# Turning expert rows on VectorE in 32x32 blocks, and one-hot products in plain fp32

## The chip, the cores and the metric

The kernel runs on one core of one Trainium2 chip. The metric is the device time of one execution, in microseconds, from the first to the last instruction and what lies around them.

## The reference

The program is two blocks, each on 512 tokens of width 1024. The first is a hybrid layer (block-sparse attention and a gated delta rule), the second a pair of token mixers followed by a layer of product-key experts. Only the last layer is touched by the change, and the norm and projection ahead of it:

```python
def peer(xn, w_q, sub_keys, u_tab, v_tab):        # u_tab, v_tab: (16384, 1024)
    q = (t @ w_q).reshape(n_tok, PEER_HEADS, 2, PEER_HALF)
    sc = jnp.einsum("thpk,hpnk->thpn", q, sub_keys)
    s_top, i_top = lax.top_k(sc, PEER_TOPK)
    ...                                           # 16 best of 16 x 16 candidates: idx, softmax g
    ue = u_tab[ib]                                # 128 rows of u for each token
    act = jax.nn.gelu(jnp.einsum("phkd,pd->phk", ue, tb))
    return jnp.einsum("phk,phkd->pd", gb * act, v_tab[ib])
```

There are 16384 experts, 128 x 128, and each token uses 128 of them (8 heads of 16).

## The kernel before

For three of the four groups of 128 tokens (384 tokens, `DENSE`) the kernel does not gather. It multiplies all experts' rows with the tokens: `u @ x` for each of 128 tiles of 128 experts, then GELU, then weighs the result with a dense table of the gate weights ("spread": experts x tokens, mostly zero), and multiplies by `v`. The last group of 128 tokens takes its rows by indirect DMA from GpSimd, one row for each token at a time, and VectorE makes the dot product with the token ("dot", 128 of them).

All large products are made of three fp32r products: an operand is split in a high part (rounded to fp32r) and a low part (the rest), and high x high, low x high and high x low are added.

The first 24 expert tiles are multiplied inside `choose_experts`, beside the top-k search. There TensorE turns a tile (8 transposes of 128x128, L1721), ScalarE copies it from PSUM twice (L1782, L1783), GpSimd makes the low part (L1832), TensorE multiplies (L1755).

The stage around the change is the first part of `expert_products`, the first expert product: 104 tiles, in rounds of four (`PER`). For tile u the steps are: SyncE loads 128 rows of 4 KB (L2058); TensorE turns them into two PSUM banks (`turn`, L2186); ScalarE writes the high part (`high`, L2401), VectorE the low part (`low`, L2260); TensorE makes 8 x 3 products of 384 columns (`multiply`, L2205); ScalarE applies GELU (L2435) and issues the store of the result (L2439).

In the first 96 tiles each tile has also one step of the spread, 4 tokens: VectorE compares key numbers with the tokens' chosen keys (`one`, L2267, and `match`, L2268), GpSimd multiplies `match` by the gate weights, high and low part (`two`, L2128), TensorE multiplies `one` and `two` (L2194), ScalarE copies the high half from PSUM into `spread` (L2408) and VectorE adds the low half (L2275). GpSimd stores finished chunks of 64 tokens to memory in 8 pieces (L2142), in half of the tiles. VectorE makes 5 dots in a round (L2280).

Each engine runs its own list in program order and waits on semaphores; there is no planner. TensorE's list is turn(u+1), multiply(u), spread step u. ScalarE's is high(u+1), GELU and store of u, spread copy of u. VectorE's is low(u+1), one-hots of u+1, dot, spread add of u. `after(n)` is n plus the one that every semaphore starts with. The second expert product (L2222, from 1662 us) and the end follow in the same block.

Of the kernel before, what the change touches and what calls it, by code (L numbers as in the profile page):

```python
# [6 lines left out]
F32 = mybir.dt.float32  # L7
# [7 lines left out]
P = 128  # L15
# [117 lines left out]

class NormAndTurn:
# [4 lines left out]
    def __init__(self, nc, k, tag, out, weight, xs, stat, rooted=False):  # L139

        self.k, self.out, self.w0, self.xs, self.stat, self.rooted = k, out, COLS[weight][0], xs, stat, rooted
        self.vec, self.sq, self.root, self.scaled, self.turned, self.his, self.los = (
            k.sem(f"{tag}_{n}") for n in ("vec", "sq", "root", "scaled", "turned", "hi", "lo"))
# [37 lines left out]
    def tensor(self, pe):  # L181
        k = self.k
        for t in range(TT):
            pe.wait_ge(self.scaled, t + 1)
            for c in range(DC):
                mm = pe.transpose(k.ps[c][:, t * P:(t + 1) * P], self.xs[t][:, c * P:(c + 1) * P], k.ident[:, :])
                if t == TT - 1:
                    mm.then_inc(self.turned, 1)
# [5 lines left out]
def project_first(nc, k, io, src, w8, proj, gates, z_raw):  # L194
# [11 lines left out]
    with ExitStack() as st:  # L206
# [18 lines left out]
        def steps_of(eng, body):  # L225
# [16 lines left out]
            k.sem(n) for n in ("rows_in", "other_rows_in", "w8_in", "ident_zero", "ident_done", "row_made", "values_set", "rows_turned", "cols_done"))  # L242

# [14 lines left out]
        with nc.Block() as block:  # L258
            @block.sync
            def _(sp):  # L260
# [1312 lines left out]
def choose_experts(nc, k, io, src, raw, chosen, rows, residual, acts, early_out):  # L1573
# [7 lines left out]
    w_dram = io["peer_wq_2"][0].rearrange("(c p) n -> p c n", p=P)  # L1581
# [8 lines left out]
    with ExitStack() as st:  # L1590
# [27 lines left out]
        u_dram = io["peer_u_2"][0].rearrange("(p c) d -> p c d", c=NKEYS)  # L1618
        flat_half = lambda ap, n: ap[:, 4 * n:4 * n + 4, :].rearrange("p c n -> p (c n)")
# [29 lines left out]
        norm = NormAndTurn(nc, k, "k_norm", src, "norm2", xs, k.norm_stat, rooted=True)  # L1649
        with nc.Block() as block:  # L1650
            @block.sync
            def _(sp):
# [18 lines left out]
                for e in range(EARLY):  # L1671
# [3 lines left out]
                    if e == EARLY - 3:  # L1675
                        sp.wait_ge(s["reduced"], after(steps))
                        for n in range(2):
                            sp.dma_start(k.xh[:, 2 + n, :], u_dram[:, EARLY + n, :]).then_inc(u_next_in, 16)
                sp.wait_ge(s["residual_out"], after(16))
                sp.wait_ge(u_next_in, after(32))  # L1680
# [4 lines left out]
            def _(pe):  # L1685
# [28 lines left out]
                def turn(e):  # L1714
# [5 lines left out]
                    for c in range(DC):  # L1720
                        mm = pe.transpose(k.ps[c // 4][:, c % 4 * P:(c % 4 + 1) * P], u_raw[e % 2][:, c * P:(c + 1) * P],  # L1721
# [239 lines left out]
def expert_products(nc, k, io, src, chosen, rows, acts, early_out, weights, spread, residual, out):  # L1961
# [8 lines left out]
    u_dram = io["peer_u_2"][0].rearrange("(p c) d -> p c d", c=NKEYS)  # L1970
# [5 lines left out]
    with ExitStack() as st:  # L1976
# [3 lines left out]
        two = [k.sb(f"u_two{b}", [P, TOK_TILE, 2, P], F32R, ctx=st) for b in range(2)]  # L1980
        match = k.sb("u_match", [P, TOK_TILE, P], ctx=st)
        weight_hi = k.sb("u_weight_hi", [P, DENSE], F32R, ctx=st)
        weight_lo = k.sb("u_weight_lo", [P, DENSE], ctx=st)
# [596 lines left out]
```

## Time and profile before

| | |
|---|---|
| median of 3 runs | 2200.09 us (2199.28 to 2201.86) |
| span of the profiled execution | 2200.7 us; the page gives no other time for it |
| mean granted TensorE clock | 0.983 |
| `choose_experts` | about 840 to 1087 us |
| first expert product, 104 tiles | 1087 to 1662 us |
| second expert product and end | 1662 to 2201 us |

A row of the timeline gives start, duration, engine, line, operation, output and inputs, and a count where like instructions are merged. Instructions of one engine overlap a little, so the distance of two starts is what one costs its engine. A plain fp32 matmul is recorded as two.

### The profile page before, as it was taken

The numbers are of one execution on the slowest core, as the hardware profiler recorded it, in microseconds if no ns is written. First come the engines' busy times: TensorE is split into PE (matmuls) and PEld (weight loads), VectorE is DVE, ScalarE is ACT, GpSimd is POOL, SyncE is SP. The second block draws the span as 40 slices with busy tenths as digits, with TensorE's granted clock in tenths as the row PEclk, the third lists the DMA queues.
The fourth block names the chain that finished last, engine by engine and source line by source line (L and its number), as shares of the span: only waits on it lengthen the run. The fifth ranks groups of instructions, "written<-read, shape, count | busy, mean of one in ns | idle before, by whom it ended". The sixth has DMA issues, their size and how long they took to land.

```text
span 2200.7 us, 35703 instructions
## 1 busy us (share of the span) xinstructions
PE 2099.8 (95%) x11175; PEld 1853.1 (84%) x11175; DVE 1692.5 (77%) x3372; ACT 828.2 (38%) x1439; POOL 773.6 (35%) x672
## 2 busy tenths in 40 slices
PE   6998988979999998999899999999999999999997
PEld 4886788758888877899899999999998888888886
DVE  3776555677778744999688888888877888888887
ACT  4454423522323224244444444444433333333333
POOL 2000044500000000334478988988743222222221
PEclk9999989989999999999999999999999999999999
DMA  6743100405234224124477988988789999999995
GB/s 136 94 59 39 20 1 20 133 14 138 69 96 111 79 82 158 58 80 142 165 245 255 320 292 285 315 284 298 256 297 343 342 335 339 338 338 338 336 340 197
DMA packets 229811, 428.46 MB, mean 195 GB/s; under 512 B 18500, under 2 KB 155876, under 8 KB 229476
## 3 DMA queue, kind: packets, MB, share of 16 engines
q1 hardware_dynamic: 173108, 255.96, 38.5%
q0 software_dynamic: 41472, 151.01, 19.9%
q10 hardware_dynamic: 15152, 20.51, 2.6%
q8 instruction: 40, 0.66, 0.1%
q14 instruction: 39, 0.32, 0.0%
HBM read 381.28 MB, written 46.14 MB: 194 GB/s over the span
## 4 chain that ended last, share of the span: by engine, by line
PE 48%; DMA 1%; DVE 1%; POOL 0%; issue 0%; SPq 0%; ACT 0%; DVEq 0%; POOLq 0%
PE bank L2222 22%; PE bank L2205 20%; PE bank L2186 4%; PE bank L2194 2%; DMA v_gg<-weights 1%; DMA acts<-u_weight_lo 0%; POOL row_slot L1957 0%; DVE u_spread L2380 0%; DVE v_residual L2370 0%; POOL u_two L2128 0%; DVE u_lo L2339 0%; DVEq L2051 0%; SPq L2066 0%; ACT u_spread L2471 0%; SPq L2062 0%
## 5 line engine op out<-in xcount | busy, mean ns | idle before, releaser
L2222 PE MATMUL bank<-u_hi,u_one 128*128 128x512 f32 x768 | 299.1, 389 | 1.6 <-DVE u_two L2342 1.5
L2222 PE MATMUL bank<-u_lo,u_one 128*128 128x512 f32 x768 | 298.8, 389 | 0.0
L2222 PE MATMUL bank<-u_hi,u_two 128*128 128x512 f32 x768 | 298.8, 389 | 0.0
L2205 PE MATMUL bank<-xt_hi,u_hi 128*128 128x384 f32 x832 | 287.1, 345 | 0.0
L2205 PE MATMUL bank<-xt_hi,u_lo 128*128 128x384 f32 x832 | 279.0, 335 | 0.0
L2205 PE MATMUL bank<-xt_lo,u_hi 128*128 128x384 f32 x832 | 278.7, 335 | 0.0
L1957 POOL DMA_INDIRECT row_slot<-in_peer_v_dram,row_index x128 | 141.1, 1102 | 388.0 <-DVE row_x L2350 365.3
L2416 ACT ACTIVATE u_hi<-xh 128x1024 fp32r<-128x1024 f32 x128 | 135.9, 1061 | 330.4 <-PE bank L2222 329.8
L2339 DVE TENSOR_TENSOR u_lo<-xh,u_hi 128x1024 fp32r<-128x1024 f32 x128 | 156.8, 1225 | 78.8 <-ACT u_hi L2416 76.0
L1641 POOL TENSOR_TENSOR k_wlo<-q_raw,k_whi 128x2048 fp32r<-128x2048 f32 x4 | 18.7, 4683 | 467.0 <-ACT k_whi L1769 467.0
L2128 POOL TENSOR_TENSOR u_two<-u_match,u_weight_hi 128x512 fp32r<-128x512 f32 x96 | 162.3, 1691 | 50.7 <-DVE u_match L2268 49.7
L1514 PE MATMUL bank<-xt_hi,x_whi 128*128 128x512 f32 x448 | 177.8, 397 | 1.6 <-DVE xt_lo L178 0.9
L1957 POOL DMA_INDIRECT row_slot<-in_peer_u_dram,row_index x128 | 160.1, 1250 | 50.8 <-issue 34.1
L1514 PE MATMUL bank<-xt_hi,x_wlo 128*128 128x512 f32 x448 | 174.4, 389 | 0.0
L1514 PE MATMUL bank<-xt_lo,x_whi 128*128 128x512 f32 x448 | 174.3, 389 | 0.0
L2222 PEld LDWEIGHTS bank<-u_hi,u_one 128*128 128x128 f32 x768 | 144.1, 188 | 32.7 <-DVE u_lo L2339 2.3
L2222 PEld LDWEIGHTS bank<-u_lo,u_one 128*128 128x128 f32 x768 | 144.2, 188 | 30.0
L2222 PEld LDWEIGHTS bank<-u_hi,u_two 128*128 128x128 f32 x768 | 144.1, 188 | 29.9
L2435 ACT ACTIVATE xh<-bank 128x384 f32<-128x384 f32 x102 | 50.2, 492 | 315.4 <-PE bank L2205 282.0
L2350 DVE SCALAR_TENSOR_TENSOR row_x<-row_slot,row_dot,row_x 128x1024 f32<-128x1024 f32 x128 | 163.7, 1279 | 0.0
L2280 DVE SCALAR_TENSOR_TENSOR row_slot<-row_slot,row_x 128x1024 f32<-128x1024 f32 x128 | 160.6, 1257 | 0.0
L2205 PEld LDWEIGHTS bank<-xt_lo,u_hi 128*128 128x128 f32 x832 | 156.9, 189 | 0.0
(440 smaller groups left out, 4947.2 us busy)
## 6 DMA issues: line engine op xcount, KB each, us to landing
xh<-in_peer_v_dram SPq DMA_DIRECT2D x128, 512.0 KB
xh<-in_peer_u_dram SPq DMA_DIRECT2D x104, 512.0 KB, 4.5
x_raw<-in_w_in_dram SPq DMA_DIRECT2D x56, 512.0 KB, 6.9
v_ga<-acts SPq DMA_DIRECT2D x128, 192.0 KB
acts<-xh ACTq DMA_DIRECT2D x102, 192.0 KB
weights<-u_spread POOLq DMA_DIRECT2D x32, 512.0 KB
v_gg<-weights SPq DMA_DIRECT2D x128, 128.0 KB
p_raw<-in_w_in_dram SPq DMA_DIRECT2D x12, 1024.0 KB, 10.2
```

Of the source, the lines that this page charges most:

```text
L1514: mm = pe.matmul(k.ps[n][:, :], w[n][:, c, :], x[:, c, :], start=(c == 0 and w is whi and x is hi), stop=(c == DC - 1 and w is wlo))
L1957: pool.indirect_dma_start(rows["slots"][slot][:, :], None, io_rows, bass.IndirectOffsetOnAxis(ap=rows["index"][:, n:n + 1], axis=0)).then_ ...
L2128: pool.tensor_tensor(two[b][:, :, h, :], match[:, :, :], part.unsqueeze(2).to_broadcast([P, TOK_TILE, P]), ALU.mult).then_inc(two_done, 1)
L2186: mm = pe.transpose(k.ps[2 * b + f][:, c % 4 * P:(c % 4 + 1) * P], raw[b][:, c * P:(c + 1) * P], k.ident[:, :])
L2194: mm = pe.matmul(k.ps[6 + q // 2][:, q % 2 * 2 * P:(q % 2 + 1) * 2 * P], one[b][:, q, :], two[b][:, q, :, :].rearrange("p h n -> p (h n)") ...
L2205: mm = pe.matmul(k.ps[4 + b][:, 0:DENSE], w[b][:, c, :], x[:, c, 0:DENSE], start=(c == 0 and w is uhi and x is hi), stop=(c == DC - 1 and ...
L2222: mm = pe.matmul(k.ps[q][:, :], h[b][:, t * P:(t + 1) * P], w[b][:, f], start=start and h is hhi and w is vhi, stop=stop and h is hlo, ski ...
L2280: dve.scalar_tensor_tensor(out=rows["slots"][slot][:, :], in0=rows["slots"][slot][:, :], scalar=1.0, in1=rows["x"][:, :], op0=ALU.mult, op ...
L2339: dve.tensor_tensor(vlo[b], v_raw[u], vhi[b].bitcast(F32), ALU.subtract).then_inc(slot_v[u], 1)
L2350: dve.scalar_tensor_tensor(out=total_of[:, :], in0=rows["slots"][u][:, :], scalar=rows["dot"][:, bass.ds(n * PER + u, 1)], in1=total_of[:, ...
L2416: act.activation(vhi[b], v_raw[u], ACT.Copy).then_inc(v["vhi_done"][b], 1)
L2435: act.activation(to, k.ps[4 + b][:, 0:DENSE], ACT.Gelu_apprx_tanh).then_inc(s["ga_done"][b], 1)
```

## The change

1. Rows are loaded in four DMAs, one for each quarter of the features (`load_turnable`): partition a*32+r gets, for each of four groups q of 32 experts, 256 features of expert row r. VectorE turns 32x32 blocks (`turn`), and its output `ut` has feature 8p+c on partition p of chunk c. So everything that is multiplied with it uses every eighth feature: the norm's turn of the tokens, the query weights, the gain columns of norm2 (loaded anew at the end of the first stage's SyncE list), and the turns of the 24 early tiles (`every_eighth`). `turn` runs two tiles ahead of the product.
2. `high` and `low` read `ut` in SBUF, one instruction each and not two.
3. `two` is plain fp32: ScalarE multiplies `match` by the weight, one copy of 128 columns for each of the four tokens (`scaled_matches`). TensorE's one-hot products are plain fp32, 128 columns, and come before the tile's product. ScalarE alone copies the result (`keep_spread`, 512 columns).
4. GpSimd only gathers and stores.

The core of the diff (the changed buffers and the waits at the switch to the second product are left out, as are the parameters that only carry the stride):

```diff
+def every_eighth(x, c):
+    return x.rearrange("p (q c) -> p c q", c=DC)[:, c, :]
+
+def load_turnable(eng, to, u_quarters, at, sem):
+    for a in range(4):
+        part = u_quarters[a][:, :, at, :].rearrange("r q o m -> r q (o m)")
+        eng.dma_start(to[a * 32:(a + 1) * 32, :].rearrange("r (q m) -> r q m", q=4), part).then_inc(sem, 16)
...
+                at, n = COLS["norm2"]
+                sp.wait_ge(cols_done, 2)
+                sp.dma_start(k.cols[:, at:at + n], io["norm2_g_2"].rearrange("a (p c) -> p (a c)", c=DC)).then_inc(norm2_in, 16)
+                sp.wait_ge(norm2_in, 16)
...
-    w_dram = io["peer_wq_2"][0].rearrange("(c p) n -> p c n", p=P)
+    w_dram = io["peer_wq_2"][0].rearrange("(p c) n -> p c n", p=P)
...
+        u_quarters = io["peer_u_2"][0].rearrange("(q r c) (a m) -> a r q c m", q=4, r=32, a=4)
...
-                        mm = pe.transpose(k.ps[c // 4][:, c % 4 * P:(c % 4 + 1) * P], u_raw[e % 2][:, c * P:(c + 1) * P],
+                        mm = pe.transpose(k.ps[c // 4][:, c % 4 * P:(c % 4 + 1) * P], every_eighth(u_raw[e % 2], c),
...
-                    sp.wait_ge(s["turned"][b], after(before * 2))
-                    sp.dma_start(raw[b], u_dram[:, bass.ds((n * PER + (u + EARLY)) % EXPERT_TILES, 1), :].rearrange("p a d -> p (a d)")
-                                 ).then_inc(s["raw_in"][b], 16)
+                    sp.wait_ge(s["turned"][b], after(before))
+                    load_turnable(sp, raw[b], u_quarters, bass.ds((n * PER + (u + EARLY)) % EXPERT_TILES, 1), s["raw_in"][b])
...
                 def spread_tokens(step, b):
                     pe.wait_ge(one_done, after(step + 1))
-                    pe.wait_ge(two_done, after(step * 2 + 2))
-                    pe.wait_ge(spread_kept, after(step * 2))
+                    pe.wait_ge(two_done, after(step + 1))
+                    pe.wait_ge(spread_kept, after(step))
                     for q in range(TOK_TILE):
-                        mm = pe.matmul(k.ps[6 + q // 2][:, q % 2 * 2 * P:(q % 2 + 1) * 2 * P], one[b][:, q, :],
-                                       two[b][:, q, :, :].rearrange("p h n -> p (h n)"), start=True, stop=True)
+                        mm = pe.matmul(k.ps[6 + b][:, q * P:(q + 1) * P], one[b][:, q, :].bitcast(F32), two[b][:, q, :],
+                                       start=True, stop=True)
...
                     for u in range(PER):
-                        if ahead(n, u):
-                            turn(n, u + 1)
-                        multiply(n, u)
                         if c is not None:
                             spread_tokens(n * PER + u, u % 2)
+                        multiply(n, u)
...
+                def turn(n, u):
+                    b, before = place(n, u)
+                    dve.wait_ge(s["raw_in"][b], after(before * 64))
+                    dve.wait_ge(s["hi_done"][b], after(before))
+                    dve.wait_ge(s["lo_done"][b], after(before))
+                    dve.transpose(ut[b].rearrange("p c (q r) -> p q c r", q=4),
+                                  raw[b].rearrange("p (q j c) -> p q c j", q=4, c=DC)).then_inc(s["turned"][b], 1)
+
                 def low(n, u):
                     b, before = place(n, u)
...
+                    dve.wait_ge(s["hi_done"][b], after(before + 1))
+                    dve.tensor_tensor(ulo[b][:, :, :], ut[b], uhi[b][:, :, :].bitcast(F32), ALU.subtract).then_inc(s["lo_done"][b], 1)
+
+                def onehots(step, b):
+                    dve.wait_ge(spread_ready, after(step - 1) if not isinstance(step, int) else max(step, 1))
+                    dve.tensor_tensor(one[b][:, :, :], keys, picks(step_at(step), 0), ALU.is_equal).then_inc(one_done, 1)
+                    dve.wait_ge(two_done, after(step))
+                    dve.tensor_tensor(match[:, :, :], keys, picks(step_at(step), 1), ALU.is_equal).then_inc(match_done, 1)
...
                     for u in range(PER):
+                        turn(n, u + 2)
                         low(n, u + 1)
...
+                        onehots(n * PER + (u + 1), (u + 1) % 2)
+                        dot(n * SLOTS + u, u, n + 1)
                     dot(n * SLOTS + PER, PER, n + 1)
...
                 def high(n, u):
                     b, before = place(n, u)
+                    act.wait_ge(s["turned"][b], after(before + 1))
                     act.wait_ge(s["product"][b], after(before))
...
+                    act.activation(uhi[b][:, :, :], ut[b], ACT.Copy).then_inc(s["hi_done"][b], 1)
+
+                def scaled_matches(step, b):
+                    act.wait_ge(match_done, after(step + 1))
+                    act.wait_ge(spread_ready, after(step - 1) if not isinstance(step, int) else max(step, 1))
+                    for q in range(TOK_TILE):
+                        at = slice(step * TOK_TILE + q, step * TOK_TILE + q + 1) if isinstance(step, int) else bass.ds(step * TOK_TILE + q, 1)
+                        ins = act.activation(two[b][:, q, :], match[:, q, :], ACT.Copy, scale=chosen[:, 2, at])
+                    ins.then_inc(two_done, 1)
+
+                def keep_spread(c, step, b):
                     act.wait_ge(spread_ready, after(step + 1))
...
+                    slots = bass.ds(step * TOK_TILE + (c % 2 * CHUNK - c * CHUNK), TOK_TILE)
+                    act.activation(spread[:, :, slots], k.ps[6 + b][:, :].rearrange("p (q n) -> p n q", q=TOK_TILE), ACT.Copy
+                                   ).then_inc(spread_kept, 1)
...
                         else:
                             act.wait_ge(spread_ready, after(steps))
                             split(0, 0)
+                        if c is not None:
+                            keep_spread(c, n * PER + u, u % 2)
+                            scaled_matches(n * PER + (u + 1), (u + 1) % 2)
                         b, before = place(n, u)
                         act.wait_ge(s["product"][b], after(before + 1))
```

## Rows read from the trace of the kernel before

**Rows 1.** The page: busy time, share of the span and instructions of each engine.
```profile
PE 2099.8 (95%) x11175; PEld 1853.1 (84%) x11175; DVE 1692.5 (77%) x3372; ACT 828.2 (38%) x1439; POOL 773.6 (35%) x672
```

**Rows 2.** The chain of waits, 1290 to 1320: start, us, what.
```profile
1296.76 0.47 PE bank L2194 x4
1297.23 0.87 PE bank L2186 x8
1298.11 4.17 PE bank L2205 x24
```

**Rows 3.** Waits of the stage, 1087 to 1665: us in total, times, longest.
```profile
PE bank L2194 <- POOL u_two L2128: 1.8, 1, 1.8
```

**Rows 4.** The timeline of ScalarE, last eight tiles: start, us, instruction.
```profile
1633.06 0.49 ACT L2435 ACTIVATE xh<-bank 128x384 f32<-128x384 f32 x1 [2.99 <-PE bank L2205]
...
1634.03 1.09 ACT L2401 ACTIVATE u_hi<-bank 128x512 fp32r<-128x512 f32 x2 [0.48 <-PE bank L2186]
...
1639.08 1.09 ACT L2401 ACTIVATE u_hi<-bank 128x512 fp32r<-128x512 f32 x2 [0.47 <-PE bank L2186]
```

**Rows 5.** The timeline of TensorE at an earlier stage's scores.
```profile
941.44 1.05 PE L1702 MATMUL bank<-k_t,k_qt 128*128 128x128 f32 x8
942.25 0.48 PE L1694 MATMUL bank<-xt_hi,k_whi 128*128 128x512 f32 x1
942.56 0.40 PE L1694 MATMUL bank<-xt_lo,k_whi 128*128 128x512 f32 x1
```

**Rows 6.** The timeline, second expert product.
```profile
1799.67 1.06 ACT L2416 ACTIVATE u_hi<-xh 128x1024 fp32r<-128x1024 f32 x1 [2.55 <-PE bank L2222]
...
1800.76 1.23 DVE L2339 TENSOR_TENSOR u_lo<-xh,u_hi 128x1024 fp32r<-128x1024 f32 x1 [0.60 <-ACT u_hi L2416]
...
1801.91 0.55 DVE L2342 TENSOR_TENSOR u_two<-v_h,u_one 128x384 fp32r<-128x384 f32 x1
```

**Rows 7.** The timeline, one tile of the first expert product.
```profile
1302.12 0.64 PE L2194 MATMUL bank<-u_two,u_one 128*128 128x256 f32 x4
...
1302.91 0.40 ACT L2408 ACTIVATE u_spread<-bank 128x256 f32 x1
...
1303.19 0.39 ACT L2408 ACTIVATE u_spread<-bank 128x256 f32 x1
...
1305.49 0.69 DVE L2267 TENSOR_TENSOR u_one<-row,chosen 128x512 fp32r<-128x512 f32 x1
...
1306.10 0.69 DVE L2268 TENSOR_TENSOR u_match<-row,chosen 128x512 f32<-128x512 f32 x1
```

**Rows 8.** The timeline of ScalarE, copies with a pointer scale.
```profile
288.89 1.14 ACT L846 ACTIVATE proj<-bank,d_small 128x128 f32 x4 [1.09 <-PE bank L886]
289.90 0.61 ACT L849 ACTIVATE x_raw<-bank 128x512 f32 x1
```

**Rows 9.** Groups of instructions: busy us, mean ns of one, idle before.
```profile
L2186 PEld LDWEIGHTS bank<-ident,xh 128*128 128x128 f32 x832 | 96.1, 143 | 4.5 <-issue 4.4
...
L1915 DVE SCALAR_TENSOR_TENSOR xh<-k_rank,k_top_f 128x256 f32<-128x256 f32 x64 | 44.8, 849 | 0.5
```

**Rows 10.** The timeline of VectorE, two dots in a row.
```profile
1635.87 1.22 DVE L2280 SCALAR_TENSOR_TENSOR row_slot<-row_slot,row_x 128x1024 f32<-128x1024 f32 x1
...
1637.01 1.22 DVE L2280 SCALAR_TENSOR_TENSOR row_slot<-row_slot,row_x 128x1024 f32<-128x1024 f32 x1
```

**Rows 11.** Stretches: length; busy (instructions) of each engine; granted clock, DMA share, GB/s.
```profile
1095.00:1101.00 6.00, 4.82 (x23) 4.83 (x24) 4.61 (x9) 1.89 (x5) 4.30 (x5) 0.72 0.94 364
1131.00:1175.00 44.00, 44.00 (x289) 44.00 (x289) 37.55 (x69) 18.19 (x40) 35.58 (x27) 1.00 0.75 251
1207.80:1251.90 44.10, 44.10 (x289) 44.10 (x288) 38.73 (x69) 18.16 (x40) 41.05 (x32) 1.00 0.98 334
```

**Rows 12.** The page, DMA issues: count, KB each, us to landing.
```profile
q_raw<-in_peer_u_dram SPq DMA_DIRECT2D x24, 512.0 KB, 3.6
q_raw<-in_peer_wq_dram SPq DMA_DIRECT2D x8, 1024.0 KB, 5.6
```

More of the change, by code:

```diff
@@ L2013, in place, with picks @@
             return u % 2, n * half + u // 2
-        def places(c, step, m):
-            slots = bass.ds(step * TOK_TILE + (2 * m - c * CHUNK + c % 2 * CHUNK), 2)
-            return spread[:, :, slots], k.ps[6 + m][:, :].rearrange("p (q h n) -> p h n q", q=2, h=2)
+        def picks(at, n):
+            return chosen[:, n, at].unsqueeze(2).to_broadcast([P, TOK_TILE, P])
+        keys = k.row[:, :].unsqueeze(1).to_broadcast([P, TOK_TILE, P])
+        step_at = lambda step: bass.ds(step * TOK_TILE, TOK_TILE) if not isinstance(step, int) else slice(step * TOK_TILE, (step + 1) * TOK_TILE)
         v_raw = [k.xh[:, u, :] for u in range(PER)]
@@ L2120, in _ @@
                 u_rows = io["peer_u_2"][0]
-                def weigh(step):
-                    b, tok = step % 2, slice(step * TOK_TILE, (step + 1) * TOK_TILE)
-                    pool.wait_ge(match_done, after(step + 1))
-                    if step >= 2:
-                        pool.wait_ge(spread_ready, after(step - 1))
-                    for h, part in enumerate((weight_hi[:, tok].bitcast(F32), weight_lo[:, tok])):
-                        pool.tensor_tensor(two[b][:, :, h, :], match[:, :, :], part.unsqueeze(2).to_broadcast([P, TOK_TILE, P]),
-                                           ALU.mult).then_inc(two_done, 1)
                 def fetch(n):
@@ L2240, in _ @@
                 for b in range(2):
[L2241 removed]
+                    pe.wait_ge(s["lo_done"][b], after(uses))
                 for u in range(PER):
@@ L2257, in low @@
                     b, before = place(n, u)
-                    for f in range(2):
-                        dve.wait_ge(s["hi_done"][b], after(before * 2 + (f + 1)))
-                        dve.tensor_tensor(ulo[b][:, 4 * f:4 * f + 4, :], k.ps[2 * b + f][:, :].rearrange("p (c n) -> p c n", c=4),
-                                          uhi[b][:, 4 * f:4 * f + 4, :].bitcast(F32), ALU.subtract).then_inc(s["lo_done"][b], 1)
-                def onehots(at, b):
-                    keys = k.row[:, :].unsqueeze(1).to_broadcast([P, TOK_TILE, P])
-                    picks = lambda n: chosen[:, n, at].unsqueeze(2).to_broadcast([P, TOK_TILE, P])
-                    dve.tensor_tensor(one[b][:, :, :], keys, picks(0), ALU.is_equal).then_inc(one_done, 1)
-                    dve.tensor_tensor(match[:, :, :], keys, picks(1), ALU.is_equal).then_inc(match_done, 1)
@@ L2270, in keep @@
-                def keep(c, step):
-                    for m in range(2):
-                        dve.wait_ge(high_kept, after(step * 2 + (m + 1)))
-                        to, parts = places(c, step, m)
-                        dve.tensor_tensor(to, to, parts[:, 1, :, :], ALU.add).then_inc(spread_kept, 1)
+                    dve.wait_ge(s["hi_done"][b], after(before + 1))
+                    dve.tensor_tensor(ulo[b][:, :, :], ut[b], uhi[b][:, :, :].bitcast(F32), ALU.subtract).then_inc(s["lo_done"][b], 1)
@@ L2297, in late_rounds @@
                     for u in range(PER):
+                        if ahead(n, u, 2):
+                            turn(n, u + 2)
                         if ahead(n, u):
@@ L2446, in _ @@
                 high(0, 0)
+                scaled_matches(0, 0)
                 for n in range(2, 4):
```

91 lines of the change are left out of this document (30 added, 61 removed).

## The prediction, made before the changed kernel was run

> **What bounds the kernel now.** I read the page's busy times first: TensorE is busy for 95% of the span [rows 1]. The chain of waits then says where: L2205 (20%), L2186 (4%) and L2194 (2%) are the first expert product, from 1087 to 1662 us. There the chain of one stretch shows a pattern that repeats with a period of 5.52 us: 4.17 us of 24 product matmuls, 0.47 us of four one-hot matmuls (L2194), 0.87 us of eight turns (L2186) [rows 2]. The waits of the stage agree: TensorE waits once for another engine's data, 1.8 us, at the start [rows 3]. In the last eight tiles, which have no one-hots, the period is 5.05 us, the distance of two ScalarE copies [rows 4]. So a shorter TensorE part gains only until some chain through the other engines is longer than what is left.
>
> **The change on TensorE.** Removed: the turns, 0.87 us per tile. The one-hot products become four plain fp32 matmuls of 128 columns each; the scores of an earlier stage are just that form: four of them (eight records, two for each) take 941.44 to 942.25, 0.81 us, and the first matmul behind them lasts 0.48 us where the next lasts 0.40, so 0.90 us in all (rounded up) against 0.47 now [rows 5]. TensorE's own work per tile is 4.17 + 0.90 = 5.07 us, 0.45 less than now, and 4.17 us in the last eight tiles. If nothing else bound, that were 96 x 0.45 + 8 x 0.88 = 50 us.
>
> **What is late next: a circle through ScalarE and VectorE.** ScalarE's order in a tile is high(u+1), keep_spread(u), scaled_matches(u+1), GELU of u and its store. VectorE's is turn(u+2), low(u+1), one-hot and match of u+1, dot.  scaled_matches(u+1) waits for match(u+1), match stands behind low(u+1), low waits for high(u+1), and high(u+1) stands behind the GELU of u-1, which stands behind scaled_matches(u). It closes once a tile, whatever TensorE does. Its links, start to start:
> GELU to high: 1633.06 to 1634.03, 0.97 us, the store's issue between them [rows 4].
> high to low: one copy of 1024 elements and the handover, 1799.67 to 1800.76, 1.09 [rows 6].
> low to one-hot: 1.15 [rows 6]. One-hot to match: 1305.49 to 1306.10, 0.61 [rows 7].
> match to scaled_matches: 0.69 [rows 7] and a handover. 0.03 us is the handover in rows 6; an instruction whose address comes from the loop's counter is later: the spread's copy starts at 1302.91, 0.15 after the one-hot matmuls' end at 1302.76 [rows 7]. I take 0.15: 0.84.
> scaled_matches to GELU: four copies of 128 columns with a pointer scale. L846 is that form, from PSUM: four of them hold ScalarE 1.01 us, from 288.89 to 289.90 [rows 8]. I take 1.01.
> Sum: 0.97 + 1.09 + 1.15 + 0.61 + 0.84 + 1.01 = 5.67 us. keep_spread hides in ScalarE's wait for match, which lasts 1.15 + 1.09 + 0.61 + 0.84 - 0.97 = 2.7 us; so does GpSimd's part, which only loses work.
> A second circle goes through TensorE in two tiles: scaled_matches(u+1) ends after 1.14 [rows 8], then 0.90 and 4.17, the GELU, and 0.97 + 1.09 + 1.15 + 0.61 + 0.84 back: 10.9 us, 5.45 a tile. So even cheaper ScalarE copies bring little below 5.45.
>
> **VectorE's turn, T.** No row shows it. Other 1024-element instructions hold VectorE 1.15 us; that is the low end (less would gain nothing, as T turns out to be free up to there). It reads single words 32 bytes apart. The nearest row with such steps is L1915, which writes 64 bytes apart: 849 ns for 256 elements [rows 9], where the slope of 1.05 ns per element between u_one (0.69, 512 elements) and u_lo (1.23, 1024) would give 0.42 [rows 6, 7]. Twice the time gives the high end, 2.5 us. I take 1.3, near the 1.15. From match to the next low lie 5.67 - 1.15 - 0.61 = 3.91 us; in them VectorE has match 0.6, a dot of 1.14 [rows 10] and T, so T is free up to 2.2 us. In every fourth tile there are two dots: 0.6 + 2.28 + 1.3 = 4.18, 0.27 over, 0.07 a tile. The period is 5.74 us. VectorE itself becomes the bound at 1.15 + 1.2 + 1.25 x 1.14 + T = 3.78 + T, beyond T of 1.95.
>
> The Trainium skill ("SBUF — State Buffer", the box on cachelines) says that accesses which step out of a 16-byte line each pay a penalty; the turn's reads do. By it, with a doubling as I would set it, T would be 2.5 and the period 6.3; that is a rival below. The skill's "Vector Engine (DVE) Microarchitecture Reference", section 3.8, has the 32x32 transpose sustain one element per cycle, which would leave T at 1.15 to 1.3. No run here shows either yet.
>
> **The clock.** TensorE would then be idle for 0.67 of 5.74 us. The granted clock is 1.00 while it is always busy [rows 11], and 0.72 in the six microseconds in which the wait of 1.8 us falls. I count that 0.67 us in each tile leave it at 1.00; if it fell by a tenth in the 5.07 us, that would lengthen the second circle to 5.7 and the forecast hardly.
>
> **Sum.** 96 tiles x (5.74 - 5.52) = +21. Last eight tiles: no one-hots; 4.17 to 4.25 against 5.05: -6.6 (zero if the loads of the second product come no earlier). Start: ahead of the first product stand two turns, low, one-hot and match, scaled_matches and the first one-hot product: 2.6 + 1.15 + 1.2 + 0.1 + 1.14 + 0.9 = 7.1 us, where a turn, high and low stand now (0.87 + 1.09 + 1.15 = 3.1). The 1.8 us wait of the start [rows 3] and the one-hot product of 0.9 are then behind it, not ahead: 7.1 - 3.1 - 1.8 - 0.9, I count +1. The earlier stage: its 24 tiles and 32 turns of the norm are still turned on TensorE, but read as every eighth element. A weight load there takes 143 ns [rows 9], beside a matmul step of about 0.11. By the doubling of L1915, all exposed, it is (192 + 32) x 0.14 = 31 us; nothing excludes zero. I take +1, since weight loads go beside matmuls. The column load of norm2 waits in SyncE's queue behind issues that are over long before their stage ends: zero. The added semaphore waits stand in front of instructions counted above. Net +16 on the profiled execution, whose span is 2200.7, 0.6 above the median shown: 2217 us; about 2216 for the median.
>
> **DMA.** Tiles with stores of the spread keep the DMA engines 98% busy, the others 75% [rows 11]. A tile's rows now come in 512 pieces of 1 KB and four issues instead of 128 of 4 KB. The loads of the query weights have 1 KB pieces: 1024 KB in 5.6 us; expert rows of 4 KB: 512 KB in 3.6 us [rows 12]. So per byte they are not slower (5.6 for twice the bytes). The load has two tiles, over 10 us, as before, and four issues a tile leave SyncE's queue mostly empty. Zero; the bound is the rival below.
>
> **Rivals.**
> 1. VectorE's turn is dear (T 2.2 to 2.6). Period 6.0 to 6.4: +46 to +85, less 5: 2240 to 2280. For: L1915. Against: slope of all plain VectorE rows. 16%.
> 2. Faster: the ScalarE circle is shorter than its rows add up to, as the four copies read SBUF and their addresses are ready beforehand. Two spread copies of 256 columns start 0.28 apart [rows 7], so 128 columns without a scale would take under 0.2: the circle is 5.67 - 0.25 - 0.12 = 5.3; TensorE's circle then holds it at 5.35 to 5.45: -12, less 6, +1: 2183 (2165 to 2196). It decides below a period of 5.50. If a link of both circles isn't there, the floor is 5.07: 2151. For: VectorE and ScalarE are far from full; against: L846 has the very form. 22%.
> 3. Small pieces make the DMA engines the bound in the 32 tiles with stores: already 98% of 5.52, that is 5.41 us of their work in a tile, and a tenth more is 5.95: 32 x 0.21 more than the forecast: 2223. 5%.
> 4. The circle comes out at 5.55 to 5.6 and all cancels: 2196 to 2205. 12%.
> The forecast, 2205 to 2240, has 45%.
> That the change doesn't take the turns off TensorE has no chance: the diff has no other user of them.
>
> **Chances and range.** What can be told from no change is about 0.2%, 4.4 us. Faster 0.22 (rival 2), the same 0.12 (rival 4), slower 0.66 (forecast, 1 and 3). The range takes the upper half of rival 2 and most of rival 1: 2188 to 2262; the forecast's own is 2205 to 2240.
>
> **What would show it.** Right: TensorE idle ahead of L2194's successor, released by ScalarE's scaled matches, 0.6 us a tile; the turn under 1.9 us; period 5.6 to 5.8; last eight tiles at 4.2; no DMA among the releasers. Wrong: a period under 5.5; VectorE without idle time (rival 1); TensorE or VectorE waiting for the rows' DMA (rival 3); in the earlier stage a period above 5.1.

## The result, and the profile after

| | before | after |
|---|---|---|
| median | 2200.65 us (2199.28 to 2201.86, 4 runs) | 2285.74 us (2281.83 to 2287.94, 4 runs) |
| ratio | | 1.0385, 95% interval 1.0371 to 1.0400 |
| span of the profiled execution | 2200.7 us | 2283.6 us |
| first expert product | 1086.7 to 1662.3 us | 1086.3 to 1742.1 us |
| distance of two GELUs, mean of 93 | 5.52 us | 6.28 us |

The change is slower by 3.85%; 2216 us was forecast, in 2188 to 2262. The sign was right, the size far too small. Of the 82.9 us between the two spans, 80.2 are the first expert product and 3.1 what follows it; the stages ahead end 0.4 earlier.

The 80.2 can be split by the GELUs of the stage, since each tile has one. The second one starts at 1103.59 before and 1113.57 after: 10.0 us, or 10.4 from the stage's start. From there to the 95th are 93 distances: 513.4 us before, 583.9 after, 70.4 more. The eight distances behind it are 41.3 and 40.3 us, so the end saves 1.0. The last GELU and the start of the second product account for the other 0.4.

Busy time of the page, which answers to [rows 1]:

```profile
PE 2077.9 (91%) x10727; PEld 1803.0 (79%) x10727; DVE 1812.4 (79%) x3178; ACT 918.0 (40%) x1627; POOL 492.1 (22%) x480
```

TensorE fell from 95% to 91% of a longer span. Which engine it waits for is told by the waits of the stage, 1086 to 1742 (engine, line, releaser: us in all, times, longest), where [rows 3] had one wait of 1.8 us:

```profile
ACT u_two L2395 <- DVE u_match L2266: 230.8, 97, 7.2
...
PE bank L2191 <- issue: 74.5, 71, 4.3
ACT u_hi L2388 <- ACT xh L2431: 63.5, 92, 0.9
DVE u_lo L2260 <- ACT u_hi L2388: 33.8, 66, 2.7
PE bank L2191 <- ACT u_two L2395: 30.3, 23, 12.0
...
DVE xh L2254 <- DMA xh<-in_peer_u_dram: 19.5, 10, 6.9
```

The scaled matches wait for `match`, `low` waits for `high`, `high` for the GELU, and TensorE for the scaled matches: the forecast circle, link by link. (Where a TensorE wait is put down to "issue", the engine had been ready for a while by the profile; it ends with the same scaled matches.) The next group is one turn of that circle, 6.00 us, on ScalarE and VectorE:

```profile
1308.02 0.47 ACT L2431 ACTIVATE xh<-bank 128x384 f32<-128x384 f32 x1
1309.16 1.06 ACT L2388 ACTIVATE u_hi<-xh 128x1024 fp32r<-128x1024 f32 x1 [0.67 <-ACT xh L2431]
1310.12 0.58 ACT L2401 ACTIVATE u_spread<-bank 128x512 f32 x1
1310.25 1.23 DVE L2260 TENSOR_TENSOR u_lo<-xh,u_hi 128x1024 fp32r<-128x1024 f32 x1 [0.52 <-ACT u_hi L2388]
1311.39 0.68 DVE L2264 TENSOR_TENSOR u_one<-row,chosen 128x512 fp32r<-128x512 f32 x1
1312.00 0.69 DVE L2266 TENSOR_TENSOR u_match<-row,chosen 128x512 f32<-128x512 f32 x1
1312.60 1.22 DVE L2271 SCALAR_TENSOR_TENSOR row_slot<-row_slot,row_x 128x1024 f32<-128x1024 f32 x1
1312.83 1.28 ACT L2395 ACTIVATE u_two<-u_match,chosen 128x128 f32<-128x128 f32 x4 [2.13 <-DVE u_match L2266]
...
1313.74 2.11 DVE L2254 STREAM_TRANSPOSE xh<-xh 128x1024 f32<-128x1024 f32 x1
1314.02 0.47 ACT L2431 ACTIVATE xh<-bank 128x384 f32<-128x384 f32 x1
```

Read the starts in order: GELU, high 1.14 later, low 1.09, one-hot 1.14, match 0.61, scaled matches 0.83, GELU 1.19. The turn (2.11 us) is nobody's wait here: it begins at 1313.74 and has to be over when the next `high` ends. In the fourth tile of a round, with two dots, it does matter, a little:

```profile
1324.53 1.22 DVE L2271 SCALAR_TENSOR_TENSOR row_slot<-row_slot,row_x 128x1024 f32<-128x1024 f32 x1
...
1325.95 0.47 ACT L2431 ACTIVATE xh<-bank 128x384 f32<-128x384 f32 x1
...
1326.82 2.21 DVE L2254 STREAM_TRANSPOSE xh<-xh 128x1024 f32<-128x1024 f32 x1
1327.34 1.06 ACT L2388 ACTIVATE u_hi<-u_ut 128x1024 fp32r<-128x1024 f32 x1 [0.92 <-ACT xh L2431]
...
1328.93 1.21 DVE L2260 TENSOR_TENSOR u_lo<-u_ut,u_hi 128x1024 fp32r<-128x1024 f32 x1
```

`high` (1327.34) would have let `low` go at 1328.43; it starts at 1328.93, behind the turn. The link from the GELU to `high` is longer here too, 1.39 us and not 1.14. And at the start of the stage the third turn stands for 6.87 us waiting for its rows, which could only be loaded once the first turn had emptied their buffer; `low` of the second tile is queued behind it:

```profile
1099.38 2.13 DVE L2254 STREAM_TRANSPOSE xh<-xh 128x1024 f32<-128x1024 f32 x1 [6.87 <-DMA xh<-in_peer_u_dram]
1101.44 1.18 DVE L2260 TENSOR_TENSOR u_lo<-u_ut,u_hi 128x1024 fp32r<-128x1024 f32 x1
```

TensorE stands idle for 4.29 us behind it, and then its clock is low: the granted clock is 0.50 from 1107 to 1110 us (the 1.2 GHz level), and matmuls of the product start 0.32 us apart, where they start 0.17 apart at 1.00:

```profile
1105.42 2.04 PE L2191 MATMUL bank<-u_two,u_one 128*128 128x128 f32 x8 [4.29 <-issue]
...
1107.58 0.52 PE L2201 MATMUL bank<-xt_lo,u_hi 128*128 128x384 f32 x1
1107.90 0.52 PE L2201 MATMUL bank<-xt_hi,u_lo 128*128 128x384 f32 x1
```

### The profile page after: what moved, and what is told of

Its sections match the earlier page's. It is cut to its first block, busy times and chain, and to the rows that moved or that the text cites. A ratio compares the mean times of both kernels' runs of the same rounds, so it can differ in the third digit from the quotient of the medians.

```text
span 2283.6 us, 35138 instructions
## 1 busy us (share of the span) xinstructions
PE 2077.9 (91%) x10727; PEld 1803.0 (79%) x10727; DVE 1812.4 (79%) x3178; ACT 918.0 (40%) x1627; POOL 492.1 (22%) x480
## 4 chain that ended last, share of the span: by engine, by line
PE 24%; DVE 9%; issue 7%; ACT 6%; DMA 4%; ACTq 1%; DVEq 1%; SPq 1%
PE bank L2215 22%; DMA xh<-in_peer_u_dram 3%; ACT u_hi L2388 3%; DVE xh L2254 2%; DVE row_slot L2271 2%; DVE u_match L2266 2%; ACT u_two L2395 2%; PE bank L2201 1%; ACTq L2433 1%; ACT xh L2431 1%; DVE u_lo L2260 1%; DVE u_one L2264 1%; SPq L143 0%; ACTq L2395 0%; DMA v_gg<-weights 0%
## 5 line engine op out<-in xcount | busy, mean ns | idle before, releaser
L2215 PE MATMUL bank<-u_hi,v_hlo 128*128 128x512 f32 x768 | 299.7, 390 | 0.0
L1976 POOL DMA_INDIRECT row_slot<-in_peer_u_dram,row_index x128 | 140.6, 1099 | 465.7 <-DVE row_slot L2271 446.4
L2395 ACT ACTIVATE u_two<-u_match,chosen 128x128 f32<-128x128 f32 x388 | 124.1, 390 | 230.8 <-DVE u_match L2266 230.8
L2191 PE MATMUL bank<-u_two,u_one 128*128 128x128 f32 x768 | 110.9, 288 | 104.8 <-issue 74.5
L2191 PEld LDWEIGHTS bank<-u_two,u_one 128*128 128x128 f32 x768 | 94.8, 194 | 132.7 <-issue 132.7
L2215 PEld LDWEIGHTS bank<-u_hi,v_hlo 128*128 128x128 f32 x768 | 144.6, 188 | 30.0
L2201 PEld LDWEIGHTS bank<-xt_hi,u_hi 128*128 128x128 f32 x832 | 158.4, 190 | 5.8 <-issue 5.8
```

The lines of the kernel that those rows point to most:

```text
L1976: pool.indirect_dma_start(rows["slots"][slot][:, :], None, io_rows, bass.IndirectOffsetOnAxis(ap=rows["index"][:, n:n + 1], axis=0)).then_ ...
L2191: mm = pe.matmul(k.ps[6 + b][:, q * P:(q + 1) * P], one[b][:, q, :].bitcast(F32), two[b][:, q, :], start=True, stop=True)
L2201: mm = pe.matmul(k.ps[4 + b][:, 0:DENSE], w[b][:, c, :], x[:, c, 0:DENSE], start=(c == 0 and w is uhi and x is hi), stop=(c == DC - 1 and ...
L2215: mm = pe.matmul(k.ps[q][:, :], h[b][:, t * P:(t + 1) * P], w[b][:, f], start=start and h is hhi and w is vhi, stop=stop and h is hlo, ski ...
L2395: ins = act.activation(two[b][:, q, :], match[:, q, :], ACT.Copy, scale=chosen[:, 2, at])
```

## The experiments

Every kernel below is the changed kernel with the edit shown, but the last, which starts from the kernel before. "Period" is the mean distance of GELUs as above, and a window is 1120 to 1560 us. The kernels were measured in several comparisons, each beside the kernel before (2199 to 2201 us), so differences between two of them are good to some 3 us.

**The order of VectorE.** Both compares go ahead of `low`, so `match` no longer stands behind `low` and `high`.

```diff
-                        low(n, u + 1)
                         onehots(n * PER + (u + 1), (u + 1) % 2)
+                        low(n, u + 1)
```

> VectorE makes the one-hots of u+1 before low(u+1), not after it; nothing else. Theory A (the circle high - low - one-hots - scaled_matches - GELU - high through ScalarE and VectorE sets the tile, 6.00 us in three tiles of four, and 6.78 in the fourth where two dots and a turn of 2.1 us lie in it): the circle is cut, and what is left is VectorE's own work, 1.15 + 1.2 + 1.25 x 1.14 + 2.08 = 5.86 us a tile; 2284 - 96 x 0.32 = 2253 us. Theory B (VectorE's amount of work alone sets the changed kernel's tile): the order is of no account, 2278 to 2288. Theory C (the rows' loads in 1 KB pieces set it): the same as B, with the waits for the rows' DMA as before, some 20 us.

Measured: 2259.95 us, 1.0275 of before (1.0245 to 1.0305); period 5.99, between theory A's 5.86 and the old 6.28, and nearer to A's.

**The turn over consecutive words.** The same instruction, all its reads and writes in a row; the features then stand in other places of the first product.

```diff
-                    dve.transpose(ut[b].rearrange("p c (q r) -> p q c r", q=4),
-                                  raw[b].rearrange("p (q j c) -> p q c j", q=4, c=DC)).then_inc(s["turned"][b], 1)
+                    dve.transpose(ut[b].rearrange("p c n -> p (c n)"), raw[b]).then_inc(s["turned"][b], 1)
```

> VectorE's turn reads and writes its 1024 elements in consecutive words (same count of 32x32 blocks; features and experts land in other places, so products are of other rows). If the 32-byte steps cost the time: the turn takes 1.2 us instead of 2.1, the fourth tile of a round falls from 6.78 to 6.0 and the total by 96 x 0.2 = 19 us, to 2265 (theory A, three tiles keep 6.00), or to 5.07 us a tile, 2176, by theory B. If the turn of 4-byte words costs it, whatever the steps: 2.1 us and 2284.

Measured: 2262.0 us, 1.0284 (1.0255 to 1.0314), theory A's time; period 6.12. The turn takes 1.24 us (shortest, median, longest in ns below), against medians of 2.08 and 2.17 in the changed kernel for the two buffers that it reads:

```profile
L2254 DVE STREAM_TRANSPOSE xh<-xh x52: 1234/1240/1246, 1088.5 to 1705.7; 128x1024 f32<-128x1024 f32 x52
```

**Hardly any turn.** It turns 32 columns in place of 1024; the rest of the turned tile is set to 1.0 once, ahead of the loop, so the product multiplies a constant.

```diff
-                    dve.transpose(ut[b].rearrange("p c (q r) -> p q c r", q=4),
-                                  raw[b].rearrange("p (q j c) -> p q c j", q=4, c=DC)).then_inc(s["turned"][b], 1)
+                    dve.transpose(ut[b][:, 0, 0:32], raw[b][:, 0:32]).then_inc(s["turned"][b], 1)
...
+                for b in range(2):
+                    dve.memset(ut[b], 1.0).then_inc(padded, 1)
```

> VectorE's turn is cut to one 32x32 block per partition group (32 columns of 1024); the rest of the turned tile is left at 1.0, so products are of constants. Theory A: the turn is out of the circle; every tile takes 6.00 us, the last eight 4.2: 2283 - 96 x 0.2 - 2 = 2262 us. Theory B: VectorE has 3.9 us a tile, so TensorE's 5.07 is the bound: 2176 us.

Measured: 2261.68 us, 1.0283 (1.0253 to 1.0313), theory A's time; period 6.10. Three tiles of a round take 6.00 to 6.03 us, as A has it, but the fourth takes 6.38 even with no turn in it.

**Rows of 4 KB.** A tile's rows come in one load, as before the change, and so the blocks stand in other places. The edit changes two things at once, the size of the pieces and the number of loads, one and not four (the turn's wait is for 16 and not 64 to match).

```diff
-                    load_turnable(sp, raw[b], u_quarters, bass.ds((n * PER + (u + EARLY)) % EXPERT_TILES, 1), s["raw_in"][b])
+                    sp.dma_start(raw[b], u_dram[:, bass.ds((n * PER + (u + EARLY)) % EXPERT_TILES, 1), :].rearrange("p a d -> p (a d)")
+                                 ).then_inc(s["raw_in"][b], 16)
```

> The rows of a tile are loaded by one DMA of 128 rows of 4 KB as in the kernel before, and turned as in the changed one (so features are mixed up). Theory A: only the waits of VectorE's turn for the rows' DMA go, 19.5 us in the trace, part of which is hidden: 2265 to 2280. Theory C: the pieces set the tile: well below, 2200 to 2230.

Measured: 2268.13 us, 1.0312 (1.0282 to 1.0342), within theory A; period 6.18.

The window of each, with its length, the busy time of PE, PEld, DVE, ACT and POOL, granted clock, DMA share and GB/s. The changed kernel:

```profile
1120.00:1560.00 440.00, 373.32 (x2240) 352.89 (x2239) 409.48 (x455) 222.36 (x486) 134.04 (x119) 1.00 0.87 254
```

The reordered compares:

```profile
1120.00:1560.00 440.00, 390.69 (x2321) 370.54 (x2320) 424.03 (x474) 236.04 (x510) 137.56 (x122) 0.98 0.91 266
```

The packed turn:

```profile
1120.00:1560.00 440.00, 381.63 (x2297) 360.20 (x2296) 360.54 (x468) 229.14 (x503) 137.49 (x122) 1.00 0.91 263
```

Hardly any turn:

```profile
1120.00:1560.00 440.00, 383.05 (x2306) 361.63 (x2305) 286.86 (x469) 230.16 (x504) 137.48 (x122) 1.00 0.95 264
```

Rows of 4 KB:

```profile
1120.00:1560.00 440.00, 377.74 (x2273) 356.66 (x2273) 416.52 (x465) 227.52 (x500) 136.73 (x122) 1.00 0.78 261
```

What follows: without its turn VectorE is busy 65% of the time and the tile still takes 6.10 us, so VectorE's load is not the bound; the circle is. The reordering cuts the circle and the period falls to 5.99 only, because there VectorE is busy 96%: its own sum is next, right below. And the turn's length is worth 0.08 us a tile in the circle (6.18 with it and almost no wait for rows, 6.10 with hardly any turn), the rows' four loads of 1 KB pieces 0.09 (6.28 against 6.18).

**Other engines make the one-hots.** First GpSimd makes `one` and `two` by itself, eight instructions of 128 columns a step; VectorE's compares and ScalarE's scaled copies are gone. Then the same with 4 KB rows.

```diff
+                    for q in range(TOK_TILE):
+                        at = slice(step * TOK_TILE + q, step * TOK_TILE + q + 1)
+                        ins = pool.tensor_scalar(one[b][:, q, :], k.row[:, :], chosen[:, 0, at], None, ALU.is_equal)
+                    ins.then_inc(one_done, 1)
+                    for q in range(TOK_TILE):
+                        at = slice(step * TOK_TILE + q, step * TOK_TILE + q + 1)
+                        ins = pool.tensor_scalar(two[b][:, q, :], k.row[:, :], chosen[:, 1, at], chosen[:, 2, at], ALU.is_equal, ALU.mult)
+                    ins.then_inc(two_done, 1)
...
-                        onehots(n * PER + (u + 1), (u + 1) % 2)
...
-                            scaled_matches(n * PER + (u + 1), (u + 1) % 2)
```

> GpSimd makes both one-hots by itself, in eight instructions of 128 columns a step (a compare with a token's key; a compare and a product with its weight), and VectorE's two compares and ScalarE's four scaled copies are gone. Theory A (in the changed kernel a circle GELU, high half, low half, compares, scaled copies, GELU sets 6.0 to 6.2 us a tile): the circle is cut, and TensorE's own work is what is left, 1.15 us for the one-hot products and 4.17 us for the product, 5.3 us a tile; with some 6.4 us a tile in the changed kernel (waits for rows in it) that is 96 times 1.0 us less, 2180 to 2195 us. GpSimd's own sum, from 460 ns for a 128x128 operation, is 3.7 us plus gathers and stores 1.9, 5.6 us; if that is the bound, 2210 to 2225 us. Theory B (rows in 1 KB pieces: 5.5 us of all 16 DMA engines a tile): the tile stays at or above 5.8 us and VectorE's turn waits for the rows, 2235 to 2260 us.

> As the kernel in which GpSimd makes the one-hots, with each tile's rows loaded in one transfer of 4 KB rows; the 32x32 blocks then stand in other places, so the first product's sums are others. If the 1 KB pieces set the tile once the circle is cut (theory B), this is 30 to 60 us faster than its sister; if TensorE or GpSimd sets it (theory A), within 10 us of it, at 2175 to 2215 us.

Measured: 2546.64 us, 1.1568 (1.1524 to 1.1612), and 2545.01 us, 1.1561 (1.1527 to 1.1594). Every range given was missed, by 290 us or more; that the two are within 10 us of each other came true. The window of the first (us busy, mean ns of one), and below it each line in the whole run (shortest, median, longest in ns):

```profile
L2165 POOL TENSOR_SCALAR u_two<-row,chosen 128x128 f32<-128x128 f32 x192 | 198.1, 1036 | 0.0
L2161 POOL TENSOR_SCALAR u_one<-row,chosen 128x128 fp32r<-128x128 f32 x191 | 140.4, 749 | 1.9
...
L2165 POOL TENSOR_SCALAR u_two<-row,chosen x388: 774/781/3692, 1096.2 to 1971.8; 128x128 f32<-128x128 f32 x194
L2161 POOL TENSOR_SCALAR u_one<-row,chosen x388: 587/601/2632, 1093.9 to 1966.0; 128x128 fp32r<-128x128 f32 x194
```

Four of each are 7.1 us a tile by the means, where I had priced all eight at 460 ns, a GpSimd operation on two tensors of that size. GpSimd is busy 424 of 440 us and the period is 9.13. The means hide two things. By the medians the two forms take 0.60 and 0.78 us, 5.5 us for the eight and not 3.7: that is the pricing. The other 1.6 us are stretched instructions, and the timeline shows beside what. Four weighted ones take 4.90 us where they meet `low` and a dot, and 3.11 alone; four plain ones take 2.44 beside a turn, which is four medians and 0.04:

```profile
1310.87 4.90 POOL L2165 TENSOR_SCALAR u_two<-row,chosen 128x128 f32<-128x128 f32 x4
1312.06 1.23 DVE L2277 TENSOR_TENSOR u_lo<-u_ut,u_hi 128x1024 fp32r<-128x1024 f32 x1 [1.33 <-ACT u_hi L2403]
1313.20 1.22 DVE L2288 SCALAR_TENSOR_TENSOR row_slot<-row_slot,row_x 128x1024 f32<-128x1024 f32 x1
...
1321.96 3.11 POOL L2165 TENSOR_SCALAR u_two<-row,chosen 128x128 f32<-128x128 f32 x4
...
1327.91 2.44 POOL L2161 TENSOR_SCALAR u_one<-row,chosen 128x128 fp32r<-128x128 f32 x4
1328.04 2.15 DVE L2271 STREAM_TRANSPOSE xh<-xh 128x1024 f32<-128x1024 f32 x1
```

Of 266 of these instructions that the window's timeline shows one by one, 193 meet no `low` and no dot of VectorE: all of them take 0.59 to 0.63 or 0.77 to 0.79 us. The 73 that meet one take up to 2.5 and 3.7: one that comes more than 0.15 us into VectorE's work on two tensors ends only after VectorE's run of such instructions has. One that begins earlier keeps its time, and then `low` is the longer (1.47 us at 1332.71, against 1.23 at 1312.06). The Trainium skill ("GPSIMD Engine Reference", section 4.1) has one-input elementwise work on GpSimd at roughly line rate. At 128 columns this trace does not show that: compare-and-multiply takes GpSimd 0.78 us alone, and VectorE 0.36 in the next kernel (a fixed part and a rate can't be told apart at one size).

**VectorE makes the weighted one-hots.** The scaled copies leave ScalarE; VectorE has four small instructions in place of `match`.

```diff
-                    dve.tensor_tensor(match[:, :, :], keys, picks(step_at(step), 1), ALU.is_equal).then_inc(match_done, 1)
+                    for q in range(TOK_TILE):
...
+                        ins = dve.tensor_scalar(two[b][:, q, :], k.row[:, :], chosen[:, 1, at], chosen[:, 2, at], ALU.is_equal, ALU.mult)
+                    ins.then_inc(two_done, 1)
...
-                            scaled_matches(n * PER + (u + 1), (u + 1) % 2)
```

> Only ScalarE's link is taken out of the circle: VectorE makes the weighted one-hots itself, four instructions of 128 columns with compare and product, in place of its one compare of 512 columns (0.61 us) and ScalarE's four copies (1.28 us). Theory A with VectorE's own sum: 2.1 turn, 1.09 low halves, 0.61 first compare, 1.6 dots, and four small ones at 0.15 to 0.3 us, 6.0 to 6.6 us a tile: no faster than the changed kernel, 2260 to 2310 us, with VectorE busy over 90% of the stage. If ScalarE's four copies alone were the fault (rival), the tile would fall by 1.2 us, to TensorE's 5.3, and the time to 2180 to 2200 us.

Measured: 2291.82 us, 1.0410 (1.0380 to 1.0441), within theory A's range; period 6.33. The window, and the small instructions in it:

```profile
1120.00:1560.00 440.00, 368.89 (x2224) 348.43 (x2223) 434.46 (x660) 144.53 (x209) 131.92 (x117) 1.00 0.87 252
...
L2267 DVE TENSOR_SCALAR u_two<-row,chosen 128x128 f32<-128x128 f32 x276 | 77.8, 359 | 0.0
```

VectorE is busy 99%. Taking ScalarE's link away from the circle gives nothing, since VectorE's sum is longer than the circle was. So a fast kernel needs both: no circle and a lighter VectorE.

**Both at once.** The reordered compares with the packed turn; then the same with 4 KB rows. The edits are those shown above. (In both the features stand in other places.)

> Two of the earlier edits together: both compares ahead of the low halves on VectorE (alone 2259.95 us, VectorE busy 96% of the stage) and the turn over consecutive words (alone 2262.0 us, VectorE busy 82%, each tile still 5.9 to 6.0 us); the words of the first product's rows stand in other places. Theory A: the first took the circle away and then met VectorE's own sum, the second took 0.85 us off that sum and then met the circle; together TensorE's 1.15 + 4.17 = 5.3 us is next, 5.3 to 5.6 us a tile, 60 to 80 us less than either alone, 2185 to 2205 us, with VectorE busy about 90%. Rival (DMA): the 1 KB pieces hold 16 engines 5.5 us a tile, tiles stay near 5.9 us and the turn waits for rows; 2240 to 2260 us.

> The same with each tile's rows in one transfer of 4 KB rows. Theory A: TensorE sets the tile in both, so it is 0 to 15 us faster than its sister (the scattered waits for rows), 2180 to 2200 us. Rival (DMA): 40 to 60 us faster than its sister.

Measured: 2211.67 us, 1.0062 of before (1.0045 to 1.0079), and 2160.18 us, 0.9821 (0.9792 to 0.9849). Alone each edit gave 24 to 26 us, together 74; the 4 KB rows, worth 18 us in the changed kernel, are worth another 51 here. The first is 7 us above theory A's range and far below its rival's; between the two kernels the DMA rival's 40 to 60 us came true, and theory A's 0 to 15 did not. The window of the first:

```profile
1120.00:1560.00 440.00, 409.44 (x2514) 401.37 (x2513) 387.94 (x511) 256.15 (x552) 151.90 (x130) 0.98 1.00 284
```

Its waits for rows there:

```profile
DVE xh L2254 <- DMA xh<-in_peer_u_dram: 24.0, 16, 3.2
DVE u_ut L2254 <- DMA xh<-in_peer_u_dram: 20.8, 10, 4.1
```

The queue that brings the rows (packets, MB, share of 16 engines):

```profile
q1 hardware_dynamic: 45075, 41.05, 39.0%
```

The window of the second, and behind it the same queue:

```profile
1120.00:1560.00 440.00, 440.00 (x2787) 439.09 (x2786) 428.86 (x567) 284.12 (x610) 167.66 (x141) 1.00 0.90 311
```
```profile
q1 hardware_dynamic: 12528, 45.62, 27.2%
```

The DMA share is 1.00 in the first: the 16 engines are full with 79 tiles in 440 us, 5.57 each, and VectorE waits 44.8 us for rows. (Whether the size of the pieces or the four loads a tile fill them is not separated; both edits go together.) By q1 the rows take 0.390 x 440 / 79 = 2.17 us of all 16 engines a tile in 1 KB pieces, and 0.272 x 440 / 87 = 1.38 in 4 KB rows, for the same 512 KB. In the second nothing waits any more but ScalarE and GpSimd, and TensorE is the bound, as its timeline shows (two lines later than in the changed kernel):

```profile
1304.33 1.05 PE L2193 MATMUL bank<-u_two,u_one 128*128 128x128 f32 x8
1305.13 0.42 PE L2203 MATMUL bank<-xt_hi,u_hi 128*128 128x384 f32 x1
1309.38 1.05 PE L2193 MATMUL bank<-u_two,u_one 128*128 128x128 f32 x8
```

0.80 + 4.25 = 5.05 us; the period is 5.06. In every kernel here that turns 4 KB rows on VectorE the features are mixed up: the turn leaves each 32x32 block on its own 32 partitions, so the pieces of a row have to be brought to different partitions by the load. The packed turn was not made for features in their right places either. The second kernel (1.8% below the kernel before) is a measure of what the change could gain, not a replacement, and the first says that with 1 KB pieces even the packed turn would be no faster than before.

**The one-hot half of the change alone, on the kernel before.** Turns stay on TensorE, GpSimd weighs once, ScalarE keeps the result. (Shown are TensorE's products alone.)

```diff
-                        mm = pe.matmul(k.ps[6 + q // 2][:, q % 2 * 2 * P:(q % 2 + 1) * 2 * P], one[b][:, q, :],
-                                       two[b][:, q, :, :].rearrange("p h n -> p (h n)"), start=True, stop=True)
+                        mm = pe.matmul(k.ps[6 + b][:, q * P:(q + 1) * P], one[b][:, q, :].bitcast(F32), two[b][:, q, :],
+                                       start=True, stop=True)
```

> The kernel before with the other half of the change alone: the turns stay on TensorE, but the one-hot products are four plain fp32 ones of 128 columns (1.15 us of records a step in the changed kernel, against 0.87 before for four of 256 columns), GpSimd weighs once a step in place of twice, and ScalarE copies the step out of one bank, VectorE's additions gone. Theory: this kernel is bound by TensorE's order (0.47 + 0.87 + 4.17 us), so the step grows by 0.25 to 0.28 us in 96 steps, 24 to 27 us, and the few waits for GpSimd go (2 us): 2220 to 2228 us. Rival: the new instructions' starts hide under the product's tail, the records only look longer: within 5 us of before. Rival: GpSimd's halved load and VectorE's missing additions let TensorE run closer: faster than before.

Measured: 2241.11 us, 1.0187 (1.0170 to 1.0204), above the 2220 to 2228 expected; period 5.93, and TensorE is busy for all of the window. One tile of it:

```profile
1305.21 1.05 PE L2189 MATMUL bank<-u_two,u_one 128*128 128x128 f32 x8
1306.11 1.04 PE L2181 MATMUL bank<-ident,xh 128*128 128x128 f32 x8
1306.90 0.42 PE L2200 MATMUL bank<-xt_hi,u_hi 128*128 128x384 f32 x1
...
1311.14 1.05 PE L2189 MATMUL bank<-u_two,u_one 128*128 128x128 f32 x8
```

0.90 + 0.79 + 4.24 = 5.93. The expectation took 0.87 for the old one-hots; that is the turns' row, the one-hots have 0.47 [rows 2]. With it the prediction's own step, 0.90 - 0.47 = 0.43 us, gives 41 us in 96 tiles; 42 were measured.

## Why the prediction was right or wrong

- **What bounds the kernel before, and TensorE's 5.07 us:** right. The one-hot product of 0.90 is measured where turns follow it, and the 5.07 as 5.05 where nothing else binds.
- **The circle as the next bound:** right in its place, order and waits; shown by the reordered compares and by the small turn.
- **Its length, 5.67 us: this step failed.** With hardly any turn the circle is 6.10, 0.43 us longer, 40 us over 93 tiles. Its six links have these means there, in the prediction's order: 1.23 + 1.09 + 1.14 + 0.60 + 0.85 + 1.19 = 6.10. Two of them are wrong, both ScalarE's. GELU to `high` was read in the last eight tiles (0.97) [rows 4]; in the tiles with a spread step it is 0.26 longer (in the changed kernel 1.14, 1.08 and 1.14 in most rounds and about 1.40 in the fourth tile, 1.21 in the mean), while in the changed kernel's own last tiles it is 0.96 to 1.10 again. The four scaled copies were priced at 1.01 by copies that read PSUM [rows 8]; from SBUF they take 1.19, 0.18 longer. The other four came out within 0.01. Why the two are longer is not shown; the first holds the issue of the store and the next tile's addresses, which differ with the place in the round.
- **T, the turn:** 2.08 to 2.17 us, not 1.3. The packed turn shows the reason: 1.24, so the 32-byte steps cost 0.84 to 0.93. The rule on cachelines of the Trainium skill ("SBUF — State Buffer", the box on cachelines) has the right sign, its doubling as I set it, 2.5, is too high; the pace of one element per cycle (the Trainium skill, "Vector Engine (DVE) Microarchitecture Reference", section 3.8) is seen only when packed. But the mis-sized T moved the time little. As the prediction had it, T is free up to about 2.2 us in three tiles of four. That the fourth's share is 0.08 us against the 0.07 forecast is luck: by the prediction's own sum a T of 2.17 would cost (0.6 + 2.28 + 2.17 - 3.91) / 4 = 0.28 us a tile, and it cost less because ScalarE's two links make the fourth tile 6.38 us long without it, and so leave the turn more room. Rival 1, which made T the price, has the right period (6.0 to 6.4) for the wrong reason. T decides only when the circle is cut.
- **DMA, "zero": failed in size.** By bytes and time to landing [rows 12] 1 KB pieces looked no slower. The time to landing is not what a load costs the engines. By queue q1 in the window that is 0.269 x 440 / 80 = 1.48 us a tile before and 0.324 x 440 / 70 = 2.04 after:

```profile
q1 hardware_dynamic: 11465, 41.79, 26.9%
...
q1 hardware_dynamic: 39745, 36.19, 32.4%
```

In the changed kernel the loads cost 0.09 us a tile, 18 us for the whole with the start (2285.74 against 2268.13, from different comparisons); hidden for the rest under the circle, and a bound of 5.54 once it is gone. Rival 3 named it, at 5%.
- **Start, +1: failed, +10.** The first product begins 5.8 us later (1095.78 against 1089.95), and the 6.87 us wait of the third turn comes on top, in part. So does the clock: after the idle 4.29 us the second tile's product takes 6.25 us (1107.12 to 1113.37), where the kernel before took 5.03 (1098.37 to 1103.40, its granted clock 0.72 from 1095 to 1101 [rows 11]) and a product at 1.00 takes 4.17. The sum had the chain of the first tile and left out the load that the third turn needs and the clock.
- **Last eight tiles, -6.6:** -1.0. Without a spread VectorE still turns, and at 1715.42 the turn waits 2.4 us for rows. **Earlier stage, +1:** -0.4. The strided weight loads there grew from 140 to 192 ns and the transposes' period did not (272 and 275 ns): hidden. **Second product, 0:** +3.1. TensorE waits 2.51 us for VectorE's low half at 1762.43, where its longest such wait was 1.09 before, and the granted clock is 0.91 from 1762 to 1782; why VectorE is late there is not shown.
- **The clock:** granted 1.00 in the window with 67 us of TensorE idle; right for the tiles, not for the start, as said.

In sum: the profiled run was forecast at 2217 and took 2283.6, 66.6 us more. The period is 6.28 - 5.74 = 0.54 us over, 50 us in 93 tiles (0.43 the links, 0.09 the pieces, 0.01 T); the start 9, the last tiles 6, the second product 3, the earlier stage -1. All but the last erred to the same side.

## What to carry to other kernels

When an engine is relieved, write the circle that closes once a tile with starts from rows of the same loop, same memory and same form; two links taken from neighbours (another part of the loop, PSUM for SBUF) cost 40 of the 67 us here. When work moves to GpSimd, ask also what VectorE runs beside it: its two-tensor instructions cost GpSimd 1.6 us a tile here. When one edit brings little, look which bound lies just beneath and lift both: edits worth 26 and 24 us alone were worth 74 together. And count a DMA by its queue's share of the 16 engines, not by how soon it lands.

## What the hardware did unexpectedly

- A 32x32-block turn of 128x1024 fp32 takes VectorE 1.24 us over consecutive words, 2.08 to 2.21 (medians) when it reads words 32 bytes apart.
- GpSimd's tensor-scalar instruction with pointer operands takes 0.60 us (one operation) and 0.78 us (two) for 128 columns, up to 2.6 and 3.7 where it meets a two-tensor instruction of VectorE, and no longer beside VectorE's turn; VectorE's with two operations takes 0.36.
- 512 KB in 1 KB pieces (four loads) hold the 16 DMA engines 2.0 to 2.3 us, in 4 KB rows (one load) 1.4 to 1.5.
- Copies of 128 columns with a pointer scale start 0.30 us apart on ScalarE from SBUF (four in 1.19), 0.25 from PSUM [rows 8].
